# Units of a layer's front handed out by need, the first branch's products inside the steps, the decays' exponentials one phase sooner

## What is computed

```python
for l in range(2):
    h = rms_norm(x, norm1_g[l])
    z = h @ w_in[l]
    (cq, ckv, kpe, gq, gk, gv, glr, gr, su, gates) = split_in(z)
    o_a = mla_mixer(cq, ckv, kpe, ...)          # attention, 8 heads, rotated q and k
    o_b = gla_mixer(gq, gk, gv, glr, gr, ...)   # linear attention: exp(bc), exp(-bc), exp(b_last - bc)
    o_c = s5_mixer(su, ...)                     # complex scan, then a product "glu"
    g = sigmoid(gates + gate_b[l])              # 3 x 1024 columns
    merged = g0 * (o_a @ w_br_mla[l]) + g1 * (o_b @ w_br_gla[l]) + g2 * (o_c @ w_br_s5[l])
    x = x + merged @ w_out[l]
    h2 = rms_norm(x, norm2_g[l])
    x = x + square(relu(h2 @ w_ff1[l])) @ w_ff2[l]
```

## Time and profile before

| | |
|---|---|
| time of three runs, median (lowest, highest) | 2615.01 us (2614.14, 2616.16) |
| the profiled execution | 2613.7 us |
| its span, first to last instruction | 2611.9 us |
| mean granted clock of PE | 0.908 |
| PE busy | 2179.4 us (83%) |
| DVE busy | 1026.4 us (39%) |
| ACT busy | 679.0 us (26%) |

### The profile page before, as it was taken

One profiled execution on the slowest core, in us unless ns is written; L12 is line 12 of the kernel. 1 busy time (PEld: TensorE's weight loads), 2 busy tenths in 40 slices (PEclk: granted clock), 3 DMA queues, 4 the chain that ended last, 5 costly groups with the idle time before them and its releaser, 6 DMA issues.

```text
span 2611.9 us, 31851 instructions
## 1 busy us (share of the span) xinstructions
PE 2179.4 (83%) x13027; PEld 1589.9 (61%) x13027; DVE 1026.4 (39%) x2106; ACT 679.0 (26%) x1048; POOL 27.3 (1%) x47
## 2 busy tenths in 40 slices
PE   7999999867667666777666588989899988899999
PEld 4886679833223333333333265778899855688999
DVE  1577865510010000101000246763664267653653
ACT  2125665300000000000000123641453125522542
POOL 0000000000000000000000010000000200000000
PEclk8999999887887888788888799999999989899999
DMA  8443544499999999999999613233355322143452
GB/s 323 150 143 133 196 155 162 198 396 421 422 389 421 421 421 421 421 421 421 421 420 422 255 48 122 99 111 129 133 190 189 114 83 104 65 160 131 158 177 101
DMA packets 174501, 631.45 MB, mean 242 GB/s; under 512 B 10816, under 2 KB 28768, under 8 KB 125200
## 3 DMA queue, kind: packets, MB, share of 16 engines
q1 hardware_dynamic: 173008, 628.07, 61.1%
q0 software_dynamic: 1344, 1.28, 0.3%
HBM read 628.28 MB, written 1.05 MB: 241 GB/s over the span
## 4 chain that ended last, share of the span: by engine, by line
PE 55%; DMA 27%; DVE 10%; ACT 4%; SPq 2%; issue 2%; DVEq 0%; ACTq 0%
DMA ring<-in_w 26%; PE pb L176 23%; PE pb L1724 5%; PE pb L1725 5%; PE pb L1726 5%; PE pb L1022 4%; PE pb L1048 3%; SPq L935 2%; DVE ar L2231 1%; PE pb L485 1%; PE pb L484 1%; PE pb L483 1%; PE pb L1681 1%; DMA ring<-in_w_ada 1%; PE pb L201 1%
## 5 line engine op out<-in xcount | busy, mean ns | idle before, releaser
L176 PE MATMUL pb<-ar,ring 128*128 128x256 f32 (+1 forms) x2960 | 673.5, 387 | 32.1 <-DVE ar L2033 18.0
L176 PEld LDWEIGHTS pb<-ar,ring 128*128 128x128 f32 (+1 forms) x2960 | 561.4, 192 | 138.6 <-issue 43.6
L1022 PE MATMUL pb<-ring,ar 128*32 128x512 f32 x2048 | 283.7, 710 | 125.0 <-DMA ring<-in_w 124.4
L1724 PE MATMUL pb<-act,parts 128*128 128x256 f32 x1152 | 331.2, 287 | 13.3 <-DVE act L2309 13.3
L1725 PE MATMUL pb<-act,parts 128*128 128x256 f32 x1152 | 327.7, 284 | 0.0
L1726 PE MATMUL pb<-act,parts 128*128 128x256 f32 x1152 | 327.6, 284 | 0.0
L1048 PE MATMUL pb<-ring,ar 128*32 128x512 f32 x1024 | 174.2, 842 | 114.2 <-DMA ring<-in_w 114.2
L1022 PEld LDWEIGHTS pb<-ring,ar 128*32 128x32 f32 x2048 | 77.6, 127 | 309.7 <-issue 309.0
L1724 PEld LDWEIGHTS pb<-act,parts 128*128 128x128 f32 x1152 | 221.7, 192 | 14.5 <-issue 14.1
L1725 PEld LDWEIGHTS pb<-act,parts 128*128 128x128 f32 x1152 | 221.6, 192 | 0.4
L1726 PEld LDWEIGHTS pb<-act,parts 128*128 128x128 f32 x1152 | 221.6, 192 | 0.0
(11 more groups left out here) (355 smaller groups left out, 2393.4 us busy)
## 6 DMA issues: line engine op xcount, KB each, us to landing
ring<-in_w SPq DMA_DIRECT2D x384, 1024.0 KB, 18.7
ring<-in_w_in SPq DMA_DIRECT2D x36, 2048.0 KB, 7.7
ring<-in_w_ff SPq DMA_DIRECT2D x32, 2048.0 KB, 8.7
ring<-in_w_ada SPq DMA_DIRECT2D x12, 2048.0 KB, 12.1
ring<-in_w_ssm_out SPq DMA_DIRECT2D x4, 2048.0 KB, 8.2
ring<-in_w_out SPq DMA_DIRECT2D x4, 2048.0 KB, 7.7
ring<-in_w_cv_out SPq DMA_DIRECT2D x2, 2048.0 KB, 8.2
ring<-in_w_mix_out SPq DMA_DIRECT2D x2, 2048.0 KB, 7.6
```

The costliest lines, as they stand in the source:

```text
L176: ins = e.matmul(out, l, r, start=(i == 0), stop=(i == len(pairs) - 1))
L1022: ins = e.matmul(k.pb[b][32 * j:32 * j + 32, :], v.xg[i][:, kt, 32 * j:32 * j + 32], w[j][:, m, :], start=(kt == 0), stop=(kt == 7))
L1724: e.matmul(k.pb[b][:, 0:T], wh[:, kt, c0:c0 + 128], xh, start=(first and kt == 0), stop=False)
```

## The change

`TILES` gives the units to the steps in another way: up to three in a step early on, none in the last eight. In all both have 31 up to gate15. Where a step has none, `upto("gate15")` only empties what is left behind on ACT. `FIRST_BRANCH` says how many of the first branch's eight products PE does in a step: one in each of steps 23 to 26, two in 27 and 28. They take their banks from the ring of the units (two banks). DVE multiplies those of a step one step later, behind its first phase; then `ff_low` of the first block of weights stands ahead of the second branch. ACT's exponentials of the decays move from the phase `prob` of the last round (step 20) to its `mask` (step 19), and DVE's three products with them from `turn_p` (step 21) to `exp` (step 20).

```diff
-TILES = [2, 2] + [1] * 27 + [0]
-
-def weave(units, main, space):
+TILES = [2, 2, 2, 3, 2, 1, 1, 3, 2, 1] + [1] * 12 + [0] * 8
+FIRST_BRANCH = [0] * 23 + [1, 1, 1, 1, 2, 2, 0]
+
+def weave(units, main, space, first_branch):
     units.upto("kpe1")
     for step, tiles in enumerate(TILES):
         main(*PHASES[2 * step])
+        first_branch(step)
         space(*SPACE[step])
-        units.more(tiles)
+        if tiles:
+            units.more(tiles)
+        else:
+            units.upto("gate15")
         main(*PHASES[2 * step + 1])
-    units.upto("gate15")
+
+def first_branch_of(step):
+    at = sum(FIRST_BRANCH[:step])
+    return range(at, at + FIRST_BRANCH[step]) if step >= 0 else range(0)
...
+    def branch(br, m, ring):
+        name, x = BRANCHES[br][0], (v.oa, v.ob, v.oc)[br]
+        w, at = landed(name, [128, 4, 1024]), 24 * l + 8 * br + m
+        e.wait_ge(*k.at(("oa", "ob", "oc")[br], (4 * l + 4, 2 * l + 2, l + 1)[br]))
+        b = ring.take(("branch", at))
+        k.group(e, k.pb[b][:, 0:T], [(w[:, i, 128 * m:128 * m + 128], x[:, i, :]) for i in range(4)]).then_inc(k.s("mm_branch"), 1)
+        ring.until(b, *k.at("branch", at + 1))
+
+    def first_branch(step):
+        for m in first_branch_of(step):
+            branch(0, m, ring)
+    weave(units, main, space, first_branch)
...
-        elif phase == "prob" and i == 3:
+        elif phase == "mask" and i == 3:
...
-        elif phase == "turn_p" and i == 3:
+        elif phase == "exp" and i == 3:
...
+    def first_branch(step):               
+        for m in first_branch_of(step - 1):
+            branch(0, m)
+
+    weave(units, main, space, first_branch)
+    first_branch(len(TILES))
...
+    ff_low(k, o, l, 0)
+    for br in (1, 2):
         for m in range(8):
+            branch(br, m)
             if br == 2 and m:
                 mg_low(m - 1)
-        if br == 0:
-            ff_low(k, o, l, 0)
         if br == 1:
             units.upto("gate23")
```

More of the change, by code:

```diff
@@ L1698, in space @@
                 ring.until(b, *k.at("glu", 4 * l + m + 1))
-    weave(units, main, space)
+    def branch(br, m, ring):
[9 more added lines that the diff above has]
+    weave(units, main, space, first_branch)
     emptied_by[4] = k.at("s5_y", 4 * l + 4)
@@ L1704, in layer_pe @@
     ring = wide
-    for br, (name, x) in enumerate(zip([b[0] for b in BRANCHES], (v.oa, v.ob, v.oc))):
-        w = landed(name, [128, 4, 1024])
-        e.wait_ge(*k.at(("oa", "ob", "oc")[br], (4 * l + 4, 2 * l + 2, l + 1)[br]))
+    for br in (1, 2):
         for m in range(8):
[L1709 to L1712, removed]
+            branch(br, m, wide)
         if br == 1:
@@ L1978, in layer_ac @@
     angle(0)
-    weave(units, main, space)
+    weave(units, main, space, lambda step: None)
     ff_high(k, o, l, 0)
@@ L2268, in layer_ve, with branch @@
     o.done(o.after(t2).tensor_tensor(v.ct[0], v.ct[0], wide[0], ALU.subtract), k.s("s5_c"))
-    weave(units, main, space)
+    def branch(br, m):
+        at = 24 * l + 8 * br + m
+        acc, g = k.pb[k.bank["branch", at]][:, 0:T], v.gate[:, (8 * br + m) % 16, :]
+        e.wait_ge(*k.at("mm_branch", at + 1))
+        after_unit(k, e, l, f"gate{8 * br + m}")
+        if br == 0:
+            o.done(e.tensor_tensor(v.mg[:, m, :], acc, g, ALU.mult), k.s("branch"))
+        else:
+            t = o.done(e.tensor_tensor(v.tmp[:, m % 2, :], acc, g, ALU.mult), k.s("branch"))
+            o.done(o.after(t).tensor_tensor(v.mg[:, m, :], v.mg[:, m, :], v.tmp[:, m % 2, :], ALU.add), k.s("mg"))
+    def first_branch(step):
[3 more added lines that the diff above has]
+    first_branch(len(TILES))
     def mg_low(m):
@@ L2273, in mg_low @@
         o.done(e.tensor_tensor(v.mgl[:, m, :], v.mg[:, m, :], v.mgh[:, m, :].bitcast(F32), ALU.subtract), k.s("mg_low"))
-    for br in range(3):
+    ff_low(k, o, l, 0)
+    for br in (1, 2):
         for m in range(8):
[L2277 to L2280, removed]
-            if br == 0:
[L2282 to L2285, removed]
+            branch(br, m)
             if br == 2 and m:
                 mg_low(m - 1)
-        if br == 0:
-            ff_low(k, o, l, 0)
         if br == 1:
```

## The result

| | before | after |
|---|---|---|
| median (lowest, highest) | 2615.01 us (2613.84, 2617.72), 7 runs | 2606.92 us (2603.98, 2609.14), 7 runs |
| ratio, 95% interval | | 0.9967 [0.9957, 0.9976] |
| the profiled execution | 2613.7 us | 2606.54 us |
| its span, mean granted clock | 2611.9 us, 0.908 | 2604.8 us, 0.915 |

The change makes the kernel 8.1 us faster; the forecast was 14.7. PE and DVE have the same work to do. In the kernel after, `weave` and what stands behind it lie some lines lower: `L1883` is now `L1902`, `L1880` is `L1899`, `L2061` is `L2080`, `L1681` is `L1693`, `L2216` is `L2235`, `L1975` is `L1994`. New names are `L2294`, DVE's product of the first branch with its gate, `L2088`, its copy of the attention's output (`keep_o`), and `L2255`, the end of its scan.

A forecast was written before the change was run, and what follows sets the result against it. PE was taken to bound both fronts. Gains of 6.4 us (front 0) and 8.3 (front 1), together 14.7, took the execution from 2613.7 to 2599.0, median 2600.3; own range 2595 to 2607, 8 in 10 range 2589 to 2612.

The forecast's parts named there:

- the walk: Step-by-step tracing of three engine queues through front 0; without clock it gave a gain of 11.7 us there.
- Steps 2 to 4: Early front 0: PE stands 4.4 us instead of 9.4; DVE's 5 us for `gv0` costs PE nothing.
- Steps 5 to 12: PE bounds front 0 here; the 6.6 us stall shrinks to 2.5 in step 7; `demod` of step 12 comes 10.5 later.
- The exponentials: Moved exponentials and DVE products fill waits before `demod` of step 21 (1703.0); front 7.3 us less late, 2.4 behind.
- Steps 22 to 28: Late front 0 without units: PE stands 6.7 us behind the reciprocals; `glu` ends at 1758.1, 2.1 us late.
- Loads: `gate16` waits for `glu` with 13.8 us of products ahead instead of 27.6; its load still fits.
- Sum: Front 0: 11.7 us without clock, 6.4 after clock and hand-overs; front 1: 8.3; together 14.7.
- B: Rival: late steps from 23 at low clock, 17 us slower, 2632 (5%); in part, 10 a front, 2614 (7%).
- C: Rival (9%): early waits for `gv0` and ACT's late emptying add 5 to 6 us to both fronts: 2611.
- D: Rival (4%): DVE and ACT bound the front throughout; products only trade places with units: 2615.

The follow-up runs named there:

- ten matmuls: The changed kernel plus ten matmuls on PE in step 28's stall, written to a free bank nobody reads: 2601.42 us.
- early emptying: The changed kernel, with DVE emptying products 4 and 5 ahead of the two reciprocals of step 28 instead of behind them: 2604.38 us.
- free banks: The changed kernel, with DVE emptying products 4 and 5 ahead of the reciprocals and `glu` taking the scan's two banks: 2589.75 us.
- the kernel with units beside the products: The changed kernel with the old `TILES` (one unit a step), keeping moved exponentials and products in the steps: 2635.52 us.

## Why the prediction was right and where it was wrong

The sign and the range held, and the walk's dates up to step 21 too, but the gain was 8.1 instead of 14.7: 2606.92 us lies at the very edge of the forecast's own 2595 to 2607. The 8.1 is a gain of 18 from one part and a loss of 10 from the others, which the forecast didn't separate. That the range held is in part luck. By the steps of the prediction, with times of front 0 set 2.64 back:

- *Steps 2 to 4.* Right. PE stands 4.67 in step 3 for ACT (forecast 4.4), and PE never waits for the rotation of k. DVE's wait for `gv0` is 8.2, not 5, and costs PE nothing, as said. The clock behind the stall was priced at 2: two units take 9.96 instead of 7.2, which is 2.8.
- *Steps 5 to 12.* The stall in step 7 is 2.51, forecast 2.5. But no clock was priced for it, and its two units take 8.76, 1.6 more. That price isn't fixed: in the second front of the same execution they take 7.17 behind the same stall (2.50), and over the two fronts of the change and its three variants (ten matmuls, early emptying, free banks) it is 8.6 to 8.8 four times and 7.17 four times. `demod` of step 12 is at 1645.2, 12.0 later than before; the forecast was 10.5 and the 2 of clock.
- *The exponentials.* Right, and shown by their own run. `demod` of step 21 is at 1704.5, forecast 1703.0 without clock.
- *Steps 22 to 28.* The step that was mis-sized. The walk made product 0 wait for the copy of o, and the outputs for the scan, but it didn't see PE stand idle there and priced no clock. Both are stalls now: 3.48 us, where the transposes of `ket` take the bank of the last attention product and the same `keep_o` empties it, and 2.02 us for the scan. Units stood there before. Behind each PE runs partly at the low level: product 0 and the outputs behind the first take 3.01 and 3.33 instead of 1.99 and 2.8, the outputs behind the second 4.23. The clock is 0.61 over the 2.95 us of product 0 and 0.83 over the 3.25 of the outputs, 0.65 over the 4.18 of the second outputs; (1 - clock) x window gives 1.7 and 1.5 us. Over the whole stretch, 1715.23 to 1769.45 us, it is 0.87, not the 0.6 throughout that the prediction gave as a sign of being wrong. The reciprocals end at 1752.6 instead of 1747.3. The last stall is 6.65, forecast 6.7; behind it products and `glu` end at 1766.8 instead of 1758.1.
- *Loads.* Right: no wait for a DMA of the weights shows in the front's list.
- *Sum.* `glu` ends 8.7 us behind the walk in front 0, and 5.3 had been priced: 2 and 3 of clock and 0.3 of hand-overs. By place: 1.5 up to `demod` of step 21, where 2 stood; 3.8 from there to the end of the reciprocals, where nothing but the 0.3 stood; 3.4 behind the last stall, where 3 stood. The missing 3.4 lie where the two short stalls stand, and their clock, 1.7 and 1.5, nearly makes them up. So the front gains 3.0, forecast 6.4; the second gains 7.4, forecast 8.3. So 4.3 of the shortfall of 6.6 lie in the two fronts. The other 2.3 lie outside them, in work that no edit touches: the profiled execution enters the first front 2.64 late, and executions of all kernels here differ by as much there.

The prediction also says that the trace has no stall between 3 and 6.6 us, and so takes the price of the one of 4.4 from the middle of a range. That holds inside the fronts, behind their first wait. In the mixture of experts there are over thirty such waits for loads, and one of 4.39 stands near the start of the execution; the clock is low behind those that were looked at: 0.83 over 8.86 us behind 4.39, 0.72 over 4.77 behind 3.44, 0.61 over 5.86 behind 4.61. They give 1.3 to 2.3 us lost, and would have said that a stall of 3.5 costs clock too.

Of the rivals, B names what happened, the late steps partly at the low clock. Its partial form had 10 a front, the forecast 5.3; the fronts end 8.7 and 6.2 us behind the walk without clock losses, between the two. C's circle of three engines was harmless in the early steps. It was real in another place, with units beside products in the late steps, and the change avoids it by having no units there. D was half true: in the late steps PE stands as long with products as without (13.3 and 13.7).

What the forecast left unasked is whether each part pays. It doesn't: the new `TILES` cost 6 us alone, and with the exponentials 11.6 (2597.0 to 2608.6); the exponentials alone would have given 18.2. The forecast's own terms had it: 7.3 a front and the 1.9 make 16.5 us for the exponentials, more than the 14.7 of the whole, so the other two parts stood at about -2 in its sum; the runs put them at -10. The early units fill the wait of 16.6 but are taken from the cover of the last eight steps. Units put right behind a wait, with the rest left in place, fill the same wait and keep the cover.

## What to carry to other kernels

Filler work is cover only where it stands: before moving it to one wait, list which waits it covers now, and test every edit of a combined change alone. Count a step's banks as queues too: a two-bank ring that another engine empties late in its own order stops the engine that fills it, and two free banks gave more here (14.6 us, 17 with the earlier emptying) than the whole change (8 us). Add to each new wait its clock, short ones included, as a range and not as one number.

## What the hardware showed

Short stalls in sparse work can already lower the granted clock. Behind a stall of 3.48 us the window has 0.81, and a product takes 3.01 us instead of 1.99; behind one of 2.02 the outputs take 4.23 instead of 2.8. In both fronts of the change and its three variants the slow stretch is there: 3.01 to 3.62 for the product, 4.23 to 4.47 for the outputs. But the length of a stall doesn't decide alone. Behind the one of 2.51 half of these fronts show no loss, and in the kernel with units beside the products the clock is 1.00 over 5.28 us behind a stall of 2.04, 0.76 over 7.01 behind one of 1.81 and 0.50 over 3.63 behind one of 2.92. What decides between them stays open.

The Trainium skill, page "TensorE: Matmul & The Clock Gate", section "A second HAM failure mode: psum-queue depth-cycling", describes short idle times between groups of matmuls that go through PSUM banks in turn, and throughput lost by the clock that falls and comes back between them. The rows behind the waits for a bank agree with it (0.81 behind 3.48 and behind 6.65); the stall of 2.02 waits for the scan's result and not for a bank.

Matmuls with no use, put into a wait that exists anyway, gave back the clock behind it: 1.00 instead of 0.81, about 2.5 us a front for ten matmuls of 0.45 us each.
